# First row products of the dense stage moved into the last block of the S5 gate stage

## The reference

```python
y = jax.nn.gelu(y + d_skip * u)
y_s5 = y * jax.nn.sigmoid(y @ w_glu) * jax.nn.silu(s5_z)
...
q = einsum('blhd,hde->bhle', heads(xc), wq)
k = einsum('blhd,hde->bhle', heads(xc), wk) * (M_HEAD_DIM ** -0.5)
v = einsum('blhd,hde->bhle', heads(m_in), wv)
o = sigmoid(einsum('blhd,hde->blhe', heads(m_in), wo))
```

## Time and profile before

| | us |
|---|---|
| runs shown | 2864.18, 2866.32 and 5423.07, median 2866.32 |
| the profiled execution's own time | 2865.76 |
| its span, first to last instruction | 2863.6 |
| PE busy in the span | 2706.9 (95%) |
| ACT, DVE, POOL busy | 1109.5, 1515.6, 468.1 |
| gate stage's last product ends | about 1152.6 after the span's start |
| dense stage, from its first instruction to its last products | 1159.1 to 1521.1 |

### The profile page before, as it was taken

The page is one execution under the profiler, slowest core; times in us unless marked ns, Lnnn a source line. Parts: engine busy times, 40 slices in busy tenths (PEclk is TensorE's granted clock), DMA queues, the critical chain, the costliest instruction groups (busy, mean ns, idle before and its releaser), DMA issues. The chain is left out here.

```text
span 2863.6 us, 37325 instructions
## 1 busy us (share of the span) xinstructions
PE 2706.9 (95%) x13471; PEld 2135.1 (75%) x13471; DVE 1515.6 (53%) x3284; ACT 1109.5 (39%) x2401; POOL 468.1 (16%) x404
## 2 busy tenths in 40 slices
PE   5899999999999899899996999998999999899999
PEld 2778887777777678678885777876787787677777
DVE  6562441566655565644544666675525441466664
ACT  3611221222222332534433555664323331466664
POOL 0003321323222000123332000000000000133332
PEclk7899999999999899999997999999999999999999
DMA  8324336444544556778886576654224433523331
GB/s 272 102 74 111 116 112 151 137 134 137 152 130 123 178 188 236 256 258 261 262 279 182 149 188 177 205 164 155 77 68 122 126 105 125 180 89 111 111 118 67
DMA packets 465994, 442.86 MB, mean 155 GB/s; under 512 B 145972, under 2 KB 362380, under 8 KB 464396
## 3 DMA queue, kind: packets, MB, share of 16 engines
q1 hardware_dynamic: 362308, 334.97, 39.3%
q10 hardware_dynamic: 103504, 105.51, 11.1%
HBM read 279.86 MB, written 161.59 MB: 154 GB/s over the span
## 5 line engine op out<-in xcount | busy, mean ns | idle before, releaser
L3079 PE MATMUL a_pg<-a_hT,a_whl 128*128 128x512 f32 x640 | 256.5, 401 | 3.4 <-DVE a_whl L922 3.4
L3081 PE MATMUL a_pg<-a_hT,a_whl 128*128 128x512 f32 x640 | 251.6, 393 | 0.0
L3080 PE MATMUL a_pg<-a_hT,a_whl 128*128 128x512 f32 x640 | 251.3, 393 | 0.0
L875 PE MATMUL pg<-hT,w_hl 128*128 128x512 f32 x512 | 205.3, 401 | 3.4 <-DVE w_hl L922 3.4
L928 PE MATMUL p_g<-hT,w_hl 128*128 128x512 f32 x512 | 203.1, 397 | 3.6 <-PEq L589 3.6
L876 PE MATMUL pg<-hT,w_hl 128*128 128x512 f32 x512 | 200.9, 392 | 0.0
L877 PE MATMUL pg<-hT,w_hl 128*128 128x512 f32 x512 | 200.9, 392 | 0.0
L930 PE MATMUL p_g<-hT,w_hl 128*128 128x512 f32 x512 | 199.6, 390 | 0.0
L929 PE MATMUL p_g<-hT,w_hl 128*128 128x512 f32 x512 | 199.4, 389 | 0.0
L3079 PEld LDWEIGHTS a_pg<-a_hT,a_whl 128*128 128x128 f32 x640 | 121.6, 190 | 42.0 <-issue 12.8
L3081 PEld LDWEIGHTS a_pg<-a_hT,a_whl 128*128 128x128 f32 x640 | 121.3, 190 | 26.2
(11 more groups left out here) (571 smaller groups left out, 6551.6 us busy)
## 6 DMA issues: line engine op xcount, KB each, us to landing
w_raw<-in_ev_w_in SPq DMA_DIRECT2D x32, 512.0 KB, 4.8
vo_d<-e_stage ACTq DMA_DIRECT2D x64, 256.0 KB, 3.8
s_wt<-s5w_d SPq DMA_DIRECT2D x32, 418.0 KB
ada_w<-in_ada_w SPq DMA_DIRECT2D x32, 384.0 KB, 6.7
shared<-h_d SPq DMA_DIRECT2D x24, 512.0 KB, 4.0
a_raw<-in_od_w_in SPq DMA_DIRECT2D x38, 256.0 KB, 3.4
gate_sums<-h_d SPq DMA_DIRECT2D x18, 512.0 KB, 3.9
arena<-in_ada_w SPq DMA_DIRECT2D x8, 1024.0 KB, 13.4
```

The lines of the kernel that those rows point to most:

```text
L875: nc.tensor.matmul(out, w[:, 0, k, :], x[:, 0, k, :], start=(k == 0), stop=False)
L3079: mm(bank, w[:, 0, k, :], x[:, 0, k, :], start=(k == 0), stop=False)
L3080: mm(bank, w[:, 0, k, :], x[:, 1, k, :], start=False, stop=False)
L3081: last = mm(bank, w[:, 1, k, :], x[:, 0, k, :], start=False, stop=(k == KC - 1))
```

## The change

Memory of the gate stage's `g_g0`, `g_g1` and `g_z` and of the dense stage's `e_x`, `e_m`, `e_y`, `e_h` and the first head's weights is placed by hand at fixed offsets above `HIGH`, so that `e_x` (`m.x_first`), `e_m` (`m.m_first`) and the first head's weights (`m.w_first`, now two tiles of two weights) exist while the gate stage runs. Four banks `e_pg` are made ahead of both stages; the gate stage uses them as its first four. The splits of the first unit, four casts on ACT and four subtractions on DVE, are taken out of the dense stage and put into the last block of the gate stage, two behind group 3's work and two behind group 5's (on ACT: behind the sigmoids and stores of its steps n = 2 and n = 4). The first four row products (24 matmuls) are issued at the end of the gate stage's PE program. The dense stage adds the counts of what was done ahead with `sem_inc` and starts PE at j = 4.

```diff
+def rows_product(nc, bank, w, x, j):
+    e = j % 2
+    for k in range(2):
+        last = split3(nc, bank, lambda q: w[0][:, q, k, j // 2, e * P:(e + 1) * P], lambda q: x[:, q, k, :], k == 0, k == 1)
+    return last
...
-        gt_high, gt_odd = sb("g_g0", [P, 4, BT]), sb("g_g1", [P, KC, BT])
+        gt_high, gt_odd = m.high("g_g0", 0, [P, 4, BT], F32), m.high("g_g1", 4, [P, KC, BT], F32)
...
+        ps = m.pg + [ctx.enter_context(nc.psum_tensor(f"g_ps{n}", [P, BT], F32)) for n in range(4, KC)]
...
+        FIRST = ((m.x_first, x_raw), (m.w_first[1], w_raw[1]), (m.w_first[0], w_raw[0]), (m.m_first, m_raw))
+        def first_hi_part(act, i):
+            if i == 0:
+                act.wait_ge(m.ahead, 16 * 6)
+                act.wait_ge(stored, (NB - 1) * KC)
+            if i == 2:
+                act.wait_ge(stored, (NB - 1) * KC + 4)
+            nc.scalar.copy(FIRST[i][0][:, 0], FIRST[i][1]).then_inc(first_hi, 1)
+        def first_lo_part(v, i):
+            v.wait_ge(first_hi, i + 1)
+            tt(FIRST[i][0][:, 1], FIRST[i][1], FIRST[i][0][:, 0].bitcast(F32), ALU.subtract).then_inc(first_lo, 1)
...
                 if b == NB - 1 and n:
                     store(act, b, n - 1)
+                    if n in (2, 4):
+                        first_hi_part(act, n - 2)
+                        first_hi_part(act, n - 1)
...
                    zt[:, n].rearrange("p (j k) -> p j k", j=CH), ALU.mult).then_inc(stored, 1)
+                if b == NB - 1 and n in (3, 5):
+                    first_lo_part(v, n - 3)
+                    first_lo_part(v, n - 2)
...
                     last.then_inc(done, 1)
+                pe.wait_ge(first_lo, 3)
+                for j in range(4):
+                    pe.wait_ge(sig, (NB - 1) * KC + j + 1)
+                    rows_product(nc, ps[j][:], m.w_first, m.x_first, j)
...
-                unit_x(0)
-                head(0, 0)
-                unit_m(0)
-                head(0, 1)
+                act.sem_inc(u_hi, 2)
+                act.sem_inc(wh_hi, 2)
...
-                unit_x(0)
-                head(0, 0)
-                unit_m(0)
-                head(0, 1)
+                v.sem_inc(u_lo, 2)
+                v.sem_inc(wh_lo, 2)
...
-                    for j in range(8):
+                    for j in range(0 if u else 4, 8):
...
+                pe.sem_inc(g_done, 4)
```

More of the change, by code:

```diff
@@ L128, in exp_steps, with split3 @@
     link(stt(out=dst, in0=n, scalar=1.0, in1=whole.bitcast(F32), op0=ALU.add, op1=ALU.mult))
+HIGH = 180192
 class Core:
     pass
+def split3(nc, bank, w, x, first, last):
+    nc.tensor.matmul(bank, w(0), x(0), start=first, stop=False)
+    nc.tensor.matmul(bank, w(0), x(1), start=False, stop=False)
+    return nc.tensor.matmul(bank, w(1), x(0), start=False, stop=last)
+def rows_product(nc, bank, w, x, j):
[3 more added lines that the diff above has]
+    return last
 def names(nc, ctx):
@@ L1298, in glu @@
         ot = [sb(f"g_o{j}", [P, BT]) for j in range(2)]
-        ps = [ctx.enter_context(nc.psum_tensor(f"g_ps{n}", [P, BT], F32)) for n in range(KC)]
+        ps = m.pg + [ctx.enter_context(nc.psum_tensor(f"g_ps{n}", [P, BT], F32)) for n in range(4, KC)]
+        assert nc.sbuf_base <= HIGH
+        first_hi, first_lo = m.sem("g_first_hi"), m.sem("g_first_lo")
         w_in = [m.sem(f"g_w_in{j}") for j in range(2)]
@@ L1310, in glu @@
         tt, stt = nc.vector.tensor_tensor, nc.vector.scalar_tensor_tensor
+        halves_of = lambda raw: [raw[:, :, 2 * j:2 * j + 2] for j in range(2)]
+        w_raw = halves_of(m.wide[:, 0:8 * HD].rearrange("p (k j e) -> p k j e", k=2, j=4))
+        x_raw, m_raw = (t[:].rearrange("p (k t) -> p k t", k=2) for t in m.bridge)
+        FIRST = ((m.x_first, x_raw), (m.w_first[1], w_raw[1]), (m.w_first[0], w_raw[0]), (m.m_first, m_raw))
[9 more added lines that the diff above has]
+            tt(FIRST[i][0][:, 1], FIRST[i][1], FIRST[i][0][:, 0].bitcast(F32), ALU.subtract).then_inc(first_lo, 1)
         def gelu(act, b, n):
@@ L1624, in dense @@
         wo_raw = m.row
-        wh = [sb(f"e_wh{j}", [P, 2, 2, 4, HD], F32R) for j in range(2)]
+        wh = [m.w_first, [sb(f"e_wh1{j}", [P, 2, 2, 2, HD], F32R) for j in range(2)]]
         wh_raw = m.wide[:, 0:8 * HD].rearrange("p (k j e) -> p k j e", k=2, j=4)
@@ L1629, in dense @@
         LASTU = UNITS - 1
-        xhl, mhl = sb("e_x", [P, 2, 2, BT], F32R), sb("e_m", [P, 2, 2, BT], F32R)
-        yhl = sb("e_y", [P, 2, KC, P], F32R)
+        xhl, mhl = m.x_first, m.m_first
+        yhl = m.high("e_y", 8, [P, 2, KC, P])
         ylast = xhl[:].rearrange("p q k t -> p q (k t)").rearrange("p q (k t) -> p q k t", t=P)
         y_of = lambda t: yhl[:] if t < LASTU else ylast
-        ht = [sb(f"e_h{j}", [P, D]) for j in range(2)]
+        ht = [m.high(f"e_h{j}", 16 + 2 * j, [P, D], F32) for j in range(2)]
         up = m.spare[:, 0:D]
@@ L1638, in dense @@
         stage = [sb(f"e_stage{j}", [P, BT]) for j in range(4)]
-        pg = [ctx.enter_context(nc.psum_tensor(f"e_pg{j}", [P, 512], F32)) for j in range(4)]
+        pg = m.pg
         po = [ctx.enter_context(nc.psum_tensor(f"e_po{j}", [P, 512], F32)) for j in range(2)]
@@ L1858, in head @@
                     v.wait_ge(wh_hi, 2 * h + j + 1)
-                    part = slice(2 * j, 2 * j + 2)
-                    sub(wh[h % 2][:, 1, :, part], wh_raw[:, :, part], wh[h % 2][:, 0, :, part]).then_inc(wh_lo, 1)
+                    sub(wh[h % 2][j][:, 1], wh_raw[:, :, 2 * j:2 * j + 2], wh[h % 2][j][:, 0]).then_inc(wh_lo, 1)
                 def unit_x(u):
@@ L1936, in _ @@
             def _(pe):
[L1937 to L1942, removed]
                 def unit(u):
@@ L1953, in unit @@
                             pe.wait_ge(g_read, g - 3)
[L1954 to L1961, removed]
+                        if j < 4:
+                            last = rows_product(nc, pg[g % 4][:], w, xhl, j)
+                        else:
+                            c = j - 4
+                            for k in range(2):
+                                last = split3(nc, pg[g % 4][:], lambda q: mhl[:, q, k, c * P:(c + 1) * P],
+                                              lambda q: w[1][:, q, k].rearrange("p a e -> p (a e)"), k == 0, k == 1)
                         last.then_inc(g_done, 1)
@@ L1970, in tile @@
                             for k in range(KC):
-                                last = split3(bank(t, n), lambda q: ylast[:, q, k, :], lambda q: wo[:, q, k, n * 512:(n + 1) * 512], k == 0, k == KC - 1)
+                                last = split3(nc, bank(t, n), lambda q: ylast[:, q, k, :], lambda q: wo[:, q, k, n * 512:(n + 1) * 512], k == 0, k == KC - 1)
                             last.then_inc(t_done, 1)
@@ L1979, in tile @@
                         for n in range(2):
-                            last = split3(po[n][:], lambda q: yhl[:, q, k, :], lambda q: wo[:, q, k, n * 512:(n + 1) * 512], k == 0, k == KC - 1)
+                            last = split3(nc, po[n][:], lambda q: yhl[:, q, k, :], lambda q: wo[:, q, k, n * 512:(n + 1) * 512], k == 0, k == KC - 1)
                     last.then_inc(t_done, 1)
+                pe.sem_inc(g_done, 4)
                 for u in range(UNITS):
@@ L3467, in trunk @@
             m.ahead_w = nc.alloc_semaphore(name="weights_ahead")
+            high = lambda n, k, s, d=F32R: nc.alloc_sbuf_tensor_at(n, s, d, offset=HIGH + 4 * BT * k)
+            m.high = high
+            m.x_first, m.m_first = high("e_x", 0, [P, 2, 2, BT]), high("e_m", 4, [P, 2, 2, BT])
+            m.w_first = [high("e_wh00", 12, [P, 2, 2, 2, HD]), high("e_wh01", 20, [P, 2, 2, 2, HD])]
+            banks = own.enter_context(ExitStack())
+            m.pg = [banks.enter_context(nc.psum_tensor(f"e_pg{j}", [P, 512], F32)) for j in range(4)]
             glu(m, a)
@@ L3476, in trunk @@
             dense(m, a)
+            banks.close()
             m.clear()
```

15 lines of the change are left out of this document (7 added, 8 removed).

## The result

The changed kernel took 2874.98 us, median of 8 runs (2871.12 to 2879.74), against 2869.34 for the kernel before; the ratio is 1.0018, 95% interval 1.0010 to 1.0027. That is 5 us slower, less than 2% and yet clear of noise; 2863.7 was forecast. The profiled execution took 2877.03 with a span of 2874.9.

The account below looks back on a forecast made before the run. PE, busy 95% of the span, was taken to bound the kernel. Tail +4.2 and head -6.8 gave -2.6 us, predicting 2863.7 from the profiled execution and the median of 2866.32; range 2859.0 to 2868.0 with rivals.

Parts of the forecast that it names:

- what the dense stage gains at its head reaches its end: Dense stage, 1250 to 1500: PE is busy for all 250 us, so no idle time there swallows a gain.
- Part 1, the tail: Gate stage's end: four subtractions in DVE's chain cost 4.6 - 0.4 = 4.2 us, bounds 4.0 and 4.9.
- Part 2: ACT's casts in the gate stage: loads there at 1139 to 1141, deadline 1144; second pair hidden with 0.8 us to spare.
- Part 3: The 24 moved matmuls at the gate stage's end: 5.4 us, ending 1160.7, hidden before the stage's new end at 1163.3.
- Rival A: Gate stage's end: all 24 moved matmuls at 0.44 us set it, +7.0 instead of +4.2; net +1.6, 2867.9; chance 0.13.
- Part 4, the head: Dense stage's start: casts, waits and half-speed products gone; gains 5.4 to 7.6 us, 6.8 taken.
- B': First dense instruction's start in the changed kernel, the gate stage's new end: 1159.14 + 4.2 = 1163.3.
- The two things that could take some back: Dense head: first store holding the fifth result, 1.2 us; unit 1's first products at lower clock, 2.1 us, 0.9 covered.
- Rival B: Output tile 0: second four weights land no earlier than 1189.58, so the gain is lost; no change, 2866.3; chance 0.10.
- Rival C: Output tile 2: PE's 2.70 us pause goes, perhaps 1.6 of slow matmuls too; 4.3 more gained, 2859.4; chance 0.12.

Follow-up runs that it names:

- pad_before: Kernel before with 384 bytes of padding ahead of e_x, e_m, e_y and everything behind them, nothing else; ratio 1.0012 against the kernel before.
- place_all: Changed kernel with HIGH = 179808 instead of 180192, so hand-placed tiles share the allocator tiles' offset within 512 bytes; 2868.33 us, ratio 0.9986 against the kernel before.
- mm_map: Separate test, not the kernel: 26 runs of 48 equal fp32r matmuls with operand addresses shifted; 11.85 us per run at shift 0, 12.14 at 32 bytes.
- cell_pad: Kernel before with 160 bytes of padding ahead of x_yhl in the cell stage; 2867.23 us, ratio 0.9983 against the kernel before.
- pool_behind_tile2: Changed kernel with HIGH = 180064, splits in idle time, y load held, x_yhl padded, POOL's second adaLN step held until tile 1 is scaled; 2854.21 us, ratio 0.9942.

## Why the prediction was wrong

- **Failed: the edit that had no term.** The change places five tiles by hand; the sum said nothing of it, and "what the dense stage gains at its head reaches its end" assumed that the dense stage keeps its pace. It did not: 0.2333 us and not 0.2267 for 16 output tiles of 48 matmuls and for 8 units of 48, 1152 * 0.0066 = 7.6 us. pad_before brings the loss into the kernel before, place_all takes it out of the changed one, mm_map shows it alone. With the 3.3 us that the seam missed (0.7 later by the steadier ruler, 2.6 earlier forecast) this is more than the 7.8 us between the forecast and the measured difference; the spread of the unchanged seam, 7.2 us at the cell stage, is wide enough for that, and no run settles it.
- **Part 1, the tail: right, mechanism and size.** 4.2 forecast; 4.2 measured from group 2's product to the end of the last group. The 4.67 from PE's last product have 0.5 of the ruler's own drift in them.
- **Part 2: right.** The loads were waited for until 1143.6, with the deadline at about 1148 in that execution (1144, and group 2's product 4.05 later than before); nothing was lost.
- **Part 3: right on the shown trace, wrong in place_all's**, where the burst at the lower level set the stage's end 1.5 us late. Rival A's mechanism exists and comes in some executions. Of the rule weighed there (the Trainium skill, TensorE: Matmul & The Clock Gate, part 1, by which the low level is the default) the two bursts show that a pause of 3 us can, and need not, bring it back.
- **Part 4, the head: mis-sized.** 6.8 was taken from a range of 5.4 to 7.6; measured 23.5 - (1187.47 - 1167.38) = 3.4, with B' = 1167.38 (POOL's first dense instruction). The two things that could take some back were named, both came, and both were larger. The fifth result came at B' + 8.5, where B' + 6.1 stood for no hold and B' + 7.3 for the hold, since the first store took 7.7 us from the first result's end and not 6.6: 2.4 lost, not 1.2. Behind a pause of 4 us PE's unit 1 took 2.7 longer at the lower clock level and j = 4 came 1.9 us late behind ACT, not 1.2 (2.1 with cover for 0.9). The two together take 7.6 down to 3.4. The prediction's own two terms give 7.6 - 1.2 - 1.2 = 5.2 for its low end, not 5.4.
- **The sum without placement.** place_all stands at 0.9986 (0.9974 to 0.9997); the forecast of -2.6 us was 0.9991, inside the interval. That is not the forecast's mechanism come true: from group 2's product to tile 1 place_all takes 65.7 us, and the four traces with the old code 65.5 to 66.0, so at the head nothing was gained. By its interval the time gained is 1 to 7 us; where it lies is open, as the cell stage starts 0.9 later than in the first trace of before and 2.7 and 6.4 earlier than in the other two.
- **Rival B fell:** ACT got the second weights 9.2 us after their issue, as before (1183.33 to 1192.50). **Rival C's pause** was 3.0 us after, 2.7 and 4.3 before and 5.1 in cell_pad. It did not go by itself, but it can be removed, and the 4.3 us at which the rival priced it is near the 4.0 that its removal gave in pool_behind_tile2.
- **The base.** The first trace of before is a lucky one: 2865.76 against a median of about 2870 to 2871.6 in all later sets. 3.6 us of that lie in the stretch of the change, by the one other trace of the same program. The forecast was a difference added to that early figure; of the 11.3 us between 2863.7 and 2874.98, 3.0 are the base (2866.32 against 2869.34).

## What to carry to other kernels

Tiles that an fp32r matmul of this shape reads together should lie at the same offset modulo 256 bytes; when an edit moves a buffer, compare the pace of the matmuls that read it (count per stretch at a busy share of 1.00), not only the idle time. Work put ahead into another stage costs nothing only where its engine idles: a pair of subtractions was free in the wait for a store and cost 2.1 us behind a later group. Before shortening a stage's head, look for what paces it next, here a store's landing; and a POOL instruction under a short DVE chain that PE waits for can be the larger prize.

## What the runs showed of the hardware that was not expected

A fp32r matmul of 128x128 by 128x512 comes every 0.2266 us when its two operands' addresses are equal modulo 256 bytes and every 0.232 to 0.234 when they are 96 or 128 apart; shifting both by the same left the pace as it was. DVE instructions of 0.28 and 0.42 us that read two SBUF tiles took 2.7 and 3.4 when they met a POOL tensor_tensor, and ended 0.13 and 0.28 behind it; the one of 1.2 us of the earlier trace rows ended 1.07 behind it, at 1234.33 against 1233.26. And pauses of PE of 2 to 4 us were followed by a slow stretch in some executions and not in others: the burst after 3.04 us of pause ran at a granted clock of 1.00, the first twelve matmuls of that after 2.89 us at half of it, with only the tiles' base address changed in the code.
